# The first expert pair's rows taken by one-hot products on TensorE instead of a gather

## Chip, core and metric

The program runs on one core of a Trainium2 chip. The time is the device time of one execution in microseconds (us); before the change it is 1830.18 us, the median of 3 runs (1829.35 to 1831.33).

## What is computed

Two layers (l = 0, 1), each on x of 512 tokens x 1024 channels in float32. Cut to what matters here, from the reference:

```python
x = x + merged @ w_out[l]
x = x + hier_moe(rmsnorm(x, norm_ffn[l]), router_group[l], ..., expert_gate[l], expert_up[l], expert_down[l])

# in hier_moe: each token goes to the two best of 32 experts (of its best group of 8)
buf = jnp.zeros((cap, D), h.dtype).at[dest].set(ht[tok_sorted])       # rows sorted by expert
out = (jax.nn.silu(xb @ w_gate[e]) * (xb @ w_up[e])) @ w_down[e]      # 1024 -> 512 -> 1024
```

## The kernel before

In each layer an attention and state-space part comes first; then `project_out_and_route` on TensorE forms `merged @ w_out` tile by tile (four tiles of 128 tokens, `out_part`, L1159), and the router works one tile behind it. VectorE adds the product into `x` (`mix_in_x`, L2101), picks the experts (`choose`) and computes for each token and each of its two experts a place: the pair (round and pair of experts, A_) and the slot of 128 in that pair (B_), in `assign`. In the last tile TensorE has nothing else to do between the steps of the router, and runs products whose result nobody reads: `keep_at_work(KEEP[i])` with `KEEP = (4, 3, 6)` (L1209).

The 32 experts are worked in 16 pairs, each with 64 slots of the 128 for each of its two experts. `tabulate` (L1202) sums one-hot products, `slot_hot` by `pair_hot`, into a table of token numbers by slot and pair. VectorE copies it out (L2192) and shifts it (L2194), and GpSimd gathers with column 0 of it the 128 rows of the first pair from `x_rows`, a copy of `x` in device memory that ScalarE's queue has written (L1444, L1448), into `xrow` (`gather`, L690). TensorE then turns the rows, eight transposes of every eighth channel each (`turn_rows`, L1249), VectorE multiplies them by the norm's gain into `xg` (`gain_rows`, L2227), four channel groups at a time, and takes each row's norm factor (`slot_root`, L2224). The expert products are L1266: gate, then up, then down, with the rows as stationary operand and weights as moving one. `xg_ready` counts four steps; the gate products of a pair wait for two of them, and their second half for all four.

Order around the change: every engine has its own program order. TensorE's is: the last tile's products, `leave` (a drain, L559), `experts`, which waits for `rows_in`, turns the rows, reads two numbers from `rounds` into registers (L1321, L1322), enters the loop and starts the gate products. SyncE issues the loads of expert weights. There are ten buffers of 2 MB; loads 0 to 9 fill them before the experts start, load 8 behind `x_out` (the copy of x is written), load 9 behind `rows_in` (the first gather has landed). Load 10 goes into the buffer of load 0 when the first half of the first gate product is done (`gate_free`), and so on (`refill`): 96 loads a layer.

The two points at which an instruction is waited for by name here:

```python
# experts(l), TensorE
pe.wait_ge(rows_in, 16)
turn_rows()
pe.wait_ge(rounds_ready, 1)
nb = pe.value_load(rounds[0:1, 0:1], min_val=1, max_val=MAXR)
# SyncE
sp.wait_ge(rows_in, 16)
load(9, 1)
```

## Time and profile before

| | |
|---|---|
| median of 3 runs | 1830.18 us |
| the profiled execution, its own time | 1827.42 us |
| its span | 1825.6 us |
| TensorE busy | 1647.8 us, 90% |
| VectorE, ScalarE, GpSimd busy | 33%, 23%, 11% |
| read from device memory | 489.25 MB |

The profiled execution took 1827.42 us, of which the span, first to last recorded instruction, is 1825.6. "Busy" of TensorE is not "needed": it counts every row that overlaps. Layer 0 has its change-over from router to experts at 431 to 449 us of the span and its experts until about 890; layer 1 the same at 1335 to 1353 and until about 1800. A row of a timeline holds the start in us, the duration in us, engine, line, operation, operands, count, and in square brackets the idle time before it and who ended it. A float32 product shows as two instructions. L554, L555 and L559 are helper lines (register steps, waits, drain), and PEldq is TensorE's sequencer.

### The profile page before, as it was taken

Reading aid. Unit: us, or ns where it says so; the run is one execution under the profiler, and the core shown is the slowest. Engines: PE = TensorE matmul, PEld = TensorE weight load, DVE = VectorE, ACT = ScalarE, POOL = GpSimd, SP = SyncE. Lnnn points to the kernel's source line nnn. Section 1 sums busy time; section 2 is a strip of 40 time slices with the busy share of each in tenths; the row PEclk is TensorE's granted clock in tenths of the full one; section 3 lists DMA queues with packets and bytes.
Section 4 is the critical chain, followed back from the end, with each engine's and each line's share of the span. In section 5 each row is a group of like instructions: output and inputs, shape, how many; then the busy total and the mean of one; then the engine's idle time right before and its main releaser. Section 6 shows DMA issues by size and latency. Waiting matters only on the chain. (4 is left out here: it accounts for less than half of the span.)

```text
span 1825.6 us, 22382 instructions
## 1 busy us (share of the span) xinstructions
PE 1647.8 (90%) x7764; PEld 863.7 (47%) x7764; DVE 596.4 (33%) x1750; ACT 411.4 (23%) x999; POOL 199.8 (11%) x283
## 2 busy tenths in 40 slices
PE   8999999999998787787999999999999978877778
PEld 6666766454443333333377577654543433323233
DVE  4885356334000000000278844553340000000003
ACT  3323555011111111111122254540111111011110
POOL 0012421000100100000000134210001100000000
PEclk9999999999999998999999999999999998999999
DMA  6631101565999999999947111026569999999998
GB/s 171 145 103 47 47 24 47 207 253 189 415 426 428 427 424 427 427 427 428 392 109 201 47 48 47 24 59 240 220 265 412 426 428 426 424 428 425 429 426 337
DMA packets 122931, 496.44 MB, mean 272 GB/s; under 512 B 42036, under 2 KB 78900, under 8 KB 94160
## 3 DMA queue, kind: packets, MB, share of 16 engines
q1 hardware_dynamic: 110608, 472.75, 65.4%
q0 software_dynamic: 8928, 16.52, 2.4%
q10 hardware_dynamic: 3296, 5.84, 0.8%
q8 instruction: 64, 1.05, 0.2%
q14 instruction: 35, 0.29, 0.0%
HBM read 489.25 MB, written 30.47 MB: 285 GB/s over the span
## 5 line engine op out<-in xcount | busy, mean ns | idle before, releaser
L1266 PE MATMUL bank<-arena 128*64 128x512 f32 x2176 | 684.4, 615 | 97.1 <-DMA arena<-in_expert_up 27.8
L1266 PEld LDWEIGHTS bank<-arena 128*64 128x64 f32 x2176 | 227.7, 141 | 356.8 <-issue 356.7
L2239 DVE SCALAR_TENSOR_TENSOR arena<-bank,halves,arena 128x512 f32<-128x512 f32 x32 | 24.0, 751 | 813.0 <-PE bank L1266 813.0
L1266 PE MATMUL bank<-h,arena 128*64 128x512 f32 x320 | 140.7, 616 | 26.5 <-DMA arena<-in_expert_gate 11.1
L1266 PE MATMUL bank<-spare_slot,arena 128*64 128x512 f32 x320 | 132.3, 611 | 29.6 <-DMA arena<-in_expert_gate 8.5
L891 PE MATMUL bank<-arena,hT 128*128 128x256 f32 (+1 forms) x512 | 119.6, 390 | 3.8 <-DMA arena<-in_w_in 2.9
L1266 PE MATMUL bank<-hT,arena 128*64 128x512 f32 x256 | 118.2, 617 | 0.0
L1159 PE MATMUL bank<-arena,hT 128*128 128x512 f32 x256 | 115.0, 597 | 0.0
L891 PEld LDWEIGHTS bank<-arena,hT 128*128 128x128 f32 x512 | 96.7, 192 | 20.5 <-issue 3.1
L1667 ACT ACT_TABLE_LOAD x32 | 41.1, 1283 | 262.4 <-PE bank L1266 262.4
L915 PE MATMUL bank<-hT,arena 128*128 128x256 f32 x384 | 97.1, 387 | 0.5 <-ACT arena L1510 0.5
L1266 PEld LDWEIGHTS bank<-h,arena 128*64 128x64 f32 x320 | 42.3, 141 | 109.6 <-issue 109.6
L1266 PEld LDWEIGHTS bank<-spare_slot,arena 128*64 128x64 f32 x320 | 40.3, 140 | 105.7 <-issue 105.7
L1669 ACT ACTIVATE arena<-bank 128x512 f32<-128x512 f32 x32 | 19.1, 597 | 295.8 <-PE bank L1303 295.8
L1552 ACT ACTIVATE arena<-bank,nbias 128x32 f32<-128x32 f32 (+4 forms) x192 | 83.4, 447 | 6.4 <-DVE nbias L2046 6.3
L891 PE MATMUL bank<-arena 128*128 128x512 f32 (+1 forms) x216 | 83.7, 551 | 0.0
L915 PEld LDWEIGHTS bank<-hT,arena 128*128 128x128 f32 x384 | 68.4, 191 | 14.8 <-issue 6.2
L915 PE MATMUL bank<-h,arena 128*128 128x256 f32 x288 | 72.0, 386 | 0.7 <-ACT spare_slot L1508 0.7
L1159 PEld LDWEIGHTS bank<-arena,hT 128*128 128x128 f32 x256 | 46.6, 190 | 49.4 <-issue 49.4
L934 PE MATMUL bank<-hT,arena 128*128 128x512 f32 x128 | 68.4, 616 | 1.5 <-ACT arena L1510 1.4
L2046 DVE TENSOR_REDUCE nbias<-bank 128x1 f32<-128x128 f32 (+3 forms) x128 | 54.8, 483 | 44.8 <-PE bank L1090 44.8
L677 POOL TENSOR_TENSOR arena<-arena 128x512 f32<-128x512 f32 x48 | 61.2, 1277 | 1.1
(382 smaller groups left out, 1936.5 us busy)
## 6 DMA issues: line engine op xcount, KB each, us to landing
arena<-in_expert_up SPq DMA_DIRECT2D x48, 2048.0 KB, 38.7
arena<-in_expert_gate SPq DMA_DIRECT2D x44, 2048.0 KB, 34.8
arena<-in_expert_down SPq DMA_DIRECT2D x44, 2048.0 KB, 39.2
arena<-in_w_in SPq DMA_DIRECT2D x26, 1024.0 KB, 5.7
spare_slot<-in_expert_gate SPq DMA_DIRECT2D x8, 2048.0 KB
h<-in_expert_gate SPq DMA_DIRECT2D x8, 2048.0 KB, 32.0
hT<-in_expert_up SPq DMA_DIRECT2D x8, 2048.0 KB, 41.4
spare_slot<-in_expert_down SPq DMA_DIRECT2D x8, 2048.0 KB
```

The lines of the kernel that those rows point to most:

```text
L677: pool.tensor_tensor(out=w[out_], in0=w[x1], in1=w[x2], op=op).then_inc(w_sums, 1)
L891: r = pe.matmul(dst, w, m, start=(i == 0), stop=(i == len(pairs) - 1))
L915: return pe.matmul(dst, w, h, start=(half == 0 and k == 0), stop=(half == 1 and k == KD // 2 - 1))
L934: r = pe.matmul(bank[:, FB, :], lhs, rhs, start=(k == 0), stop=(k == n - 1))
L1159: r = pe.matmul(bank[:, c, :], mergedT[:, k, P * t:P * t + P], w_o[:, c, k, :], start=(k == 0), stop=(k == KD - 1))
L1266: r = pe.matmul(dst[CAP * e:CAP * e + CAP, :], moving[:, k, CAP * e:CAP * e + CAP], w, start=(k == 0), stop=(k == n - 1))
L1552: act.activation(p, s, ACT.Exp, scale=-1.0, bias=nbias[:, n % 2, i:i + 1], accum_out=rsum[:, n % 2, i:i + 1])\
L1667: act.activation(hid, bank[:, 2, :], ACT.Silu, scale=slot_root).then_inc(silu_done, 1)
L1669: act.activation(actT.rearrange("p a b -> p (a b)"), bank[:, 6, :], ACT.Copy).then_inc(at_ready, 1)
L2046: dve.tensor_reduce(nbias[:, n % 2, i:i + 1], bank[:, i, 0:nk], AX.X, ALU.min).then_inc(max_ready, 1)
L2239: STT(hid, bank[:, 3, :], slot_root, hid, ALU.mult, ALU.mult).then_inc(act_ready, 1)
```

## The change

The first pair is no longer gathered. For every tile VectorE computes `first_slot` = 128 A_ + B_, which is below 128 only for places in round 0, pair 0, and from it a one-hot matrix of token by slot, `row_hot`. TensorE multiplies it (as stationary operand) with `x` (moving, 512 wide, in an order that puts channels 8p + k together for each k) over the four tiles, in two halves of the channels, and with the column of norm factors. ScalarE copies both halves to `xrow`, TensorE turns them with eight transposes of neighbouring columns (`turn_first`), VectorE applies the gain. These products stand where `keep_at_work` stood, and `keep_at_work` is gone. The table's last tile, copy and shift come later, since only the second pair needs them. The two numbers of `rounds` are computed and read earlier. `slot_hot` and `pair_hot` have one buffer in place of two, the table's products go to bank 3. Loads 8 and 9 lose their waits. TensorE's wait `enter(pe, exp_clear, l)` stands ahead of `project_out_and_route`. Every other pair is gathered as before.

```diff
@@ GpSimd
                 pool.wait_ge(table_ready, 1)
                 pool.wait_ge(x_out, 32 * NT)
-                gather(table[:, 1, 0:1])
                 pool.wait_ge(xg_ready, 4)
                 gather(table[:, 1, 1:2])
@@ SyncE
                 leave(sp, left_mix)
-                sp.wait_ge(x_out, 32 * NT)
                 load(8, 1)
-                sp.wait_ge(rows_in, 16)
                 load(9, 1)
@@ TensorE
-            def keep_at_work(n):
-
-                for i in range(n):
-                    pe.matmul(bank[:, 3, :], ident[:, :], x[:, i % NT, 0:512], start=True, stop=True)
+            def first_rows(c, *tiles):
+
+                for t in tiles:
+                    pe.wait_ge(hot_ready, t + 1)
+                    r = pe.matmul(bank[:, c, :], row_hot[:, t, :],
+                                  x[:, t, :].rearrange("q (p k) -> q k p", k=KD)[:, 4 * c:4 * c + 4, :],
+                                  start=(t == 0), stop=(t == NT - 1))
+                    if t == NT - 1:
+                        r.then_inc(rows_mm, 1)
+
+            def first_roots(*tiles):
+
+                for t in tiles:
+                    r = pe.matmul(bank[:, 6, P:P + 1], row_hot[:, t, :], row_root[:, t, 0:1],
+                                  start=(t == 0), stop=(t == NT - 1))
+                    if t == NT - 1:
+                        r.then_inc(roots_mm, 1)
+
+            def turn_first(c):
+
+                pe.wait_ge(rows_copied, c + 1)
+                for k in range(4):
+                    o = 512 * c + P * k
+                    r = pe.transpose(bank[:, c, P * k:P * k + P], xrow[:, o:o + P], ident[:, :])
+                r.then_inc(xt_done, 1)
...
                 logits(t, 1)
-                keep_at_work(KEEP[0])
+                first_rows(0, 0, 1, 2)
+                first_rows(1, 0)
                 prefix(t)
-                keep_at_work(KEEP[1])
-                tabulate(t)
-                keep_at_work(KEEP[2])
+                first_rows(1, 1, 2)
+                first_roots(0, 1, 2)
+                first_rows(0, t)
+                first_rows(1, t)
+                first_roots(t)
...
-                pe.wait_ge(rows_in, 16)
-                turn_rows()
                 pe.wait_ge(rounds_ready, 1)
                 nb = pe.value_load(rounds[0:1, 0:1], min_val=1, max_val=MAXR)
                 earlier = pe.value_load(rounds[0:1, 1:2], min_val=0, max_val=PAIRS * (MAXR - 1))
+                turn_first(0)
+                tabulate(NT - 1)
+                turn_first(1)
@@ ScalarE
+                for c in range(2):
+                    act.wait_ge(rows_mm, c + 1)
+                    act.activation(xrow[:, 512 * c:512 * c + 512], bank[:, c, :], ACT.Copy).then_inc(rows_copied, 1)
                 act.wait_ge(r_exp_in, 1)
@@ VectorE
                     do(STT(pl(A_), pl(ROUND_), float(PAIRS), pl(PAIR), ALU.mult, ALU.add))
+                    do(STT(first_slot[:, t, :], pl(A_), float(P), pl(B_), ALU.mult, ALU.add))
+                    do(TS(row_hot[:, t, :], iota_f[:, :], first_slot[:, t, 0:1], None, ALU.is_equal))
+                    STT(row_hot[:, t, :], iota_f[:, :], first_slot[:, t, 1:2], row_hot[:, t, :], ALU.is_equal, ALU.add)\
+                        .then_inc(hot_ready, 1)
...
+                one_hots(NT - 1)
+                dve.wait_ge(roots_mm, 1)
+                dve.tensor_copy(slot_root, bank[:, 6, P:P + 1]).then_inc(xg_ready, 1)
+                dve.wait_ge(xt_done, 1)
+                gain_rows(0)
+                dve.wait_ge(table_mm, NT)
...
+                dve.wait_ge(xt_done, 2)
+                dve.sem_inc(xg_ready, 1)
+                gain_rows(1)
+                TS(table[:, 1, :], table[:, 0, :], 1, None, ALU.logical_shift_right).then_inc(table_ready, 1)
```

TensorE's order between the last `prefix` and the first expert product, first before (L1209 the idle products, L1202 the table, L1249 the transposes of the gathered rows, L1321 and L1322 the register loads):

```order
L1209 MATMUL bank<-x,ident 128x512 x3
L1202 MATMUL bank<-arena 128x128 [waits slots_ready] x2
L1209 MATMUL bank<-x,ident 128x512 x6
L1249 MATMUL bank<-ident,arena 128x128 [waits exp_clear,rows_in]
L1249 MATMUL bank<-ident,arena 128x128 x7
L1321 TENSOR_LOAD rounds [waits rounds_ready]
L1321 ISA x2
L1322 TENSOR_LOAD rounds
L1322 ISA x2
L1323 UNCONDITIONAL_BRANCH
L1323 ISA
L554 ISA [waits xg_ready]
```

The same stretch of the changed kernel (L1212 `first_rows`, L1221 `first_roots`, L1345 and L1346 the register loads, L1231 `turn_first`, L1204 the table):

```order
L1212 MATMUL bank<-x,arena 128x512 [waits hot_ready] x2
L1221 MATMUL bank<-arena 128x1
L1345 TENSOR_LOAD rounds [waits rounds_ready]
L1345 ISA x2
L1346 TENSOR_LOAD rounds
L1346 ISA x2
L1231 MATMUL bank<-ident,arena 128x128 [waits rows_copied]
L1231 MATMUL bank<-ident,arena 128x128 x3
L1204 MATMUL bank<-arena 128x128 [waits slots_ready] x2
L1231 MATMUL bank<-ident,arena 128x128 [waits rows_copied]
L1231 MATMUL bank<-ident,arena 128x128 x3
L1350 UNCONDITIONAL_BRANCH
```

The register loads have moved ahead of the transposes, and the table's last tile between the two groups of transposes.

VectorE's order behind the last `assign`, before (L2168, L2170 `slot_hot` and `pair_hot`):

```order
L2166 SCALAR_TENSOR_TENSOR place<-place 128x2
L2168 TENSOR_SCALAR arena<-iota_f,place 128x128 [waits dve_chain]
L2170 TENSOR_SCALAR arena<-iota_f,place,row_f 128x128
L2168 TENSOR_SCALAR arena<-iota_f,place 128x128
L2170 TENSOR_SCALAR arena<-iota_f,place,row_f 128x128
L2190 TENSOR_REDUCE cnt<-bank 128x1
L2192 TENSOR_SCALAR table<-bank 128x128 [waits table_mm,dve_chain]
```

And of the changed kernel (L2196 to L2198 the new one-hot, L2206 and L2208 the old two):

```order
L2195 SCALAR_TENSOR_TENSOR place<-place 128x2
L2196 SCALAR_TENSOR_TENSOR first_slot<-place 128x2 [waits dve_chain]
L2197 TENSOR_SCALAR arena<-iota_f,first_slot 128x128 [waits dve_chain]
L2198 SCALAR_TENSOR_TENSOR arena<-iota_f,first_slot,arena 128x128 [waits dve_chain]
L2233 TENSOR_REDUCE cnt<-bank 128x1
L2234 TENSOR_SCALAR cnt<-thr,cnt 128x8 [waits dve_chain]
L2235 TENSOR_REDUCE cnt<-cnt 128x1 [waits dve_chain]
L2236 TENSOR_SCALAR cnt<-cnt 128x1 [waits dve_chain]
L2237 TENSOR_SCALAR cnt<-cnt 128x1
L2238 CAST rounds<-cnt 128x2 [waits dve_chain]
L2206 TENSOR_SCALAR arena<-iota_f,place 128x128 [waits table_mm]
L2208 TENSOR_SCALAR arena<-iota_f,place,row_f 128x128
```

The new one-hot comes first, then the round numbers, and only then the operands of the table.

## Rows read from the trace of the kernel before

**Rows 1.** Windows: length, PE, PEld, DVE, ACT, POOL busy, PEclk, DMA share, GB/s

```profile
458.00:474.00 16.00, 14.58 (x72) 6.40 (x70) 2.01 (x4) 1.79 (x3) 1.24 (x3) 1.00 1.00 427
474.00:880.00 406.00, 335.82 (x1502) 136.63 (x1500) 28.09 (x56) 52.07 (x69) 32.73 (x54) 0.95 1.01 425
```

**Rows 2.** The chain that ended last, layer 1's experts: start us, us, what

```profile
1441.88 13.97 PE bank L1266 x64
1456.50 39.46 DMA arena<-in_expert_down
...
1732.22 42.69 DMA arena<-in_expert_down
```

**Rows 3.** Timeline of SyncE's queue, layer 0: loads 8, 9, 10, and 14 with 15

```profile
436.54 0.33 SPq L809 DMA_DIRECT2D arena<-in_expert_up  x1
446.08 0.33 SPq L809 DMA_DIRECT2D hT<-in_expert_up  x1
452.82 0.36 SPq L809 DMA_DIRECT2D spare_slot<-in_expert_down  x1
...
473.17 0.84 SPq L809 DMA_DIRECT2D arena<-in_expert_up  x2
```

**Rows 4.** Timeline of TensorE, the change-over of layer 0, and last of layer 1

```profile
434.05 3.68 PE L1209 MATMUL bank<-x,ident 128*128 128x512 f32 x8
...
437.93 2.82 PE L1209 MATMUL bank<-x,ident 128*128 128x512 f32 x6
...
446.62 1.14 PE L1249 MATMUL bank<-ident,arena 128*128 128x128 f32 x8 [0.26 <-issue]
448.75 3.65 PE L1266 MATMUL bank<-spare_slot,arena 128*64 128x512 f32 x16 [1.00 <-DVE arena L2227]
...
1352.42 3.65 PE L1266 MATMUL bank<-spare_slot,arena 128*64 128x512 f32 x16 [0.80 <-DVE halves L2224]
```

**Rows 5.** TensorE's sequencer by line, 430 to 460 us: ns, start us

```profile
L559 PEldq DRAIN  x1: 5598/5598/5598, 440.8 to 440.8; - x1
...
L1321 PEldq TENSOR_LOAD <-rounds x1: 489/489/489, 446.7 to 446.7; - x1
...
L1322 PEldq SEQ_ASSERT  x1: 18/18/18, 448.1 to 448.1; - x1
```

**Rows 6.** Timeline of VectorE in layer 0's last two tiles

```profile
412.61 0.69 DVE L2101 SCALAR_TENSOR_TENSOR x<-bank,x 128x512 f32<-128x512 f32 x1 [1.88 <-PE bank L1159]
...
439.20 0.17 DVE L2164 TENSOR_SCALAR place<-place 128x2 f32<-128x2 f32 x1
439.40 0.16 DVE L2165 SCALAR_TENSOR_TENSOR place<-place 128x2 f32<-128x2 f32 x1
...
439.67 0.29 DVE L2168 TENSOR_SCALAR arena<-iota_f,place 128x128 f32<-128x128 f32 x1
...
440.32 0.34 DVE L2170 TENSOR_SCALAR arena<-iota_f,place,row_f 128x128 f32<-128x128 f32 x1
...
447.34 0.69 DVE L2227 TENSOR_TENSOR arena<-bank,g_ffn 128x512 f32<-128x512 f32 x1 [1.67 <-PE bank L1249]
```

**Rows 7.** ScalarE's copies of a bank, by line: ns min/median/max

```profile
L1440 ACT ACTIVATE arena<-bank x14: 591/597/597, 381.3 to 1331.4; 128x512 f32<-128x512 f32 x14
```

**Rows 8.** Weight loads by line and shape: busy us, mean ns of one

```profile
L1249 PEld LDWEIGHTS bank<-ident,arena 128*128 128x128 f32 x256 | 31.0, 193 | 26.4 <-issue 24.3 <-DMA arena<-x_rows,table 2.1
...
L1118 PEld LDWEIGHTS bank<-arena,h 128*64 128x64 f32 x320 | 16.7, 135 | 23.2 <-DVE arena L2072 14.0 <-issue 5.4 <-ACT arena L1562 2.7
...
L975 PEld LDWEIGHTS bank<-arena 128*63 128x63 f32 x128 | 10.3, 205 | 20.2 <-issue 20.2
...
L1170 PEld LDWEIGHTS bank<-ident,x 128*128 128x128 f32 x64 | 7.5, 141 | 5.3 <-issue 4.2 <-DVE x L2101 1.1
```

**Rows 9.** Windows around one pair's transposes, and TensorE behind a long wait

```profile
484.00:490.00 6.00, 4.50 (x26) 2.37 (x23) 2.01 (x4) 0.60 (x1) 0.18 (x1) 1.00 1.02 434
...
603.64 1.08 PE L1266 MATMUL bank<-h,arena 128*64 128x512 f32 x1 [3.03 <-DMA arena<-in_expert_gate]
```

More of the change, by code:

```diff
@@ L70 @@
 NRING = 4
-KEEP = (4, 3, 6)
 PLAIN = 2
@@ L306, in trunk @@
         junk = view(112, 512)
-        slot_hot = view(107, 2, 2, P)
-        pair_hot = view(109, 2, 2, P)
+        slot_hot = view(107, 2, P)
+        pair_hot = view(108, 2, P)
+        row_hot = view(109, NT, P)
         ident = sb("ident", [P, P])
@@ L358, in trunk @@
         table = sb("table", [P, 2, P], I32)
+        first_slot = sb("first_slot", [P, NT, 2])
         slot_tok = sb("slot_tok", [P, 1], I32)
@@ L448, in trunk @@
         member_ready = sem("member_ready")
-        slots_ready = sem("slots_ready")
-        table_mm = sem("table_mm")
+        slots_ready = sem("slots_ready", "exp")
+        table_mm = sem("table_mm", "exp")
+        hot_ready = sem("hot_ready", "exp")
+        rows_mm = sem("rows_mm", "exp")
+        roots_mm = sem("roots_mm", "exp")
+        rows_copied = sem("rows_copied", "exp")
         table_ready = sem("table_ready", "exp")
@@ L727, in _ @@
                 pool.sem_inc(yslot_free, 1)
-                wait_reg(pool, rows_in, earlier * 16 + 16 * PAIRS)
+                wait_reg(pool, rows_in, earlier * 16 + 16 * (PAIRS - 1))
                 pool.dma_reset()
@@ L1298, in pair @@
                     else:
-                        wait_reg(pe, rows_in, it * 16 + 32)
+                        wait_reg(pe, rows_in, it * 16 + 16)
                         turn_rows()
@@ L1660, in _ @@
                 leave(act, left_mix)
+                act.wait_ge(x_out, 32 * NT)
                 act.wait_ge(rounds_ready, 1)
@@ L2183, in _ @@
                         assign(t - 1)
+                        one_hots(t - 1)
                     mix_in_x(t, 1)
@@ L2190, in _ @@
                 do(dve.tensor_reduce(cnt[:, 8:9], bank[:, 6 + (NT - 1) % 2, 96:96 + NE], AX.X, ALU.max))
-                dve.wait_ge(table_mm, NT)
-                do(TS(table[:, 0, :].rearrange("p (h w v) -> p h w v", h=4, w=4),
-                      bank[:, 2, 0:P].rearrange("p (h v w) -> p h w v", h=4, w=4), float(EMPTY), None, ALU.add))
-                TS(table[:, 1, :], table[:, 0, :], 1, None, ALU.logical_shift_right).then_inc(table_ready, 1)
                 do(TS(cnt[:, 0:8], thr[:, :], cnt[:, 8:9], None, ALU.is_lt))
@@ L2197, in _ @@
                 link(TS(cnt[:, 10:11], cnt[:, 9:10], 1.0, None, ALU.add))
+                do(TS(cnt[:, 11:12], cnt[:, 9:10], float(PAIRS), None, ALU.mult))
+                dve.tensor_copy(rounds[:, :], cnt[:, 10:12]).then_inc(rounds_ready, 1)
+                one_hots(NT - 1)
[4 more added lines that the diff above has]
+                dve.wait_ge(table_mm, NT)
+                do(TS(table[:, 0, :].rearrange("p (h w v) -> p h w v", h=4, w=4),
+                      bank[:, 3, 0:P].rearrange("p (h v w) -> p h w v", h=4, w=4), float(EMPTY), None, ALU.add))
+                dve.wait_ge(xt_done, 2)
+                dve.sem_inc(xg_ready, 1)
+                gain_rows(1)
+                TS(table[:, 1, :], table[:, 0, :], 1, None, ALU.logical_shift_right).then_inc(table_ready, 1)
                 link(TS(cnt[:, 12:13], cnt[:, 9:10], float(PAIRS), float(PAIRS - 1), ALU.mult, ALU.add))
-                do(TS(cnt[:, 11:12], cnt[:, 9:10], float(PAIRS), None, ALU.mult))
-                dve.sem_inc(xg_ready, 1)
-                dve.tensor_copy(rounds[:, :], cnt[:, 10:12]).then_inc(rounds_ready, 1)
                 for t in range(NT):
@@ L2224, in root_rows @@
                     dve.tensor_copy(slot_root, xrow[:, D:D + 1]).then_inc(xg_ready, 1)
-                def gain_rows(q):
-                    TT(xg[:, 4 * q:4 * q + 4, :], bank[:, q, :].rearrange("p (k c) -> p k c", k=4),
-                       bc(g_ffn[:, 4 * q:4 * q + 4], P), ALU.mult).then_inc(xg_ready, 1)
-                for q in range(2):
-                    dve.wait_ge(xt_done, q + 1)
-                    gain_rows(q)
-                    if q == 0:
-                        root_rows()
                 def gated(it):
```

16 lines of the change are left out of this document (10 added, 6 removed).

## Prediction

> **What bounds the kernel now.** I read four views, from the whole to the place. The windows first: in layer 0's experts the DMA engines are busy at 1.00 of their time and move 427 GB/s from 458 us on, and 425 GB/s for the next 406 us, while TensorE is busy for 336 of those 406 [rows 1]. So the experts' end is set by when the stream of weights gets going, not by TensorE's speed in the middle. The chain that ended last says the same: TensorE's products up to 1456 us, and from there to the last load at 1732 one DMA wait after another, 39 to 43 us from issue to landing [rows 2], which is the time that a full set of buffers takes.
>
> What starts that stream is in SyncE's queue. Loads 0 to 9 fill the ten buffers. Load 10 is issued at 452.82, four microseconds behind the first gate product at 448.75 [rows 3, 4], because it needs the buffer that the first half of that product frees. Loads 14 and 15 come at 473.17, when pair 0 is done. From load 10 on 86 loads are still to be moved, whatever happened before. If the first expert product starts a given time earlier, load 10 and all releases of pair 0 do too, and the layer ends that much earlier. Layer 1 has the same structure, with its first expert product at 1352.42. So the question is what ends last before 448.75.
>
> Load 9 is issued when the first gather has landed: 446.08 [rows 3]. But the idle products end only with the drain, at 440.8 + 5.6 = 446.4 [rows 5]. The transposes start at 446.62 [rows 4]. TensorE's sequencer reads the two numbers from 446.7 to 448.1 [rows 5], and the first gate product starts at 448.75. VectorE's gain, 447.34 + 0.69 = 448.03 [rows 6], was there 0.7 earlier. So the chain is: router, table, gather (with the idle products 0.3 longer still), transposes issued, register loads (1.4), loop entry (0.6).
>
> **The change, part by part.**
>
> VectorE. Before, the one-hots start at 439.67 [rows 6]. Now `first_slot` stands there, a small dependent operation: 0.20, the distance of two such (439.20 to 439.40). Then a 128-wide comparison whose end is waited for, 0.29 and some 0.04, and a 128-wide one with two tensor inputs, which the trace does not show with this operation; I take 0.34, the dearer 128-wide row [rows 6]; between 0.29 and 0.69 (a 512-wide one) it can cost 0.05 less or 0.35 more. `hot_ready` comes at 439.67 + 0.20 + 0.33 + 0.34 = 440.54. In the earlier tiles these 0.9 us fall into VectorE's wait for TensorE, 1.88 us in the row shown [rows 6]; were it gone, they would cost 0.9 three times a layer.
>
> TensorE, hidden part. The idle products were 4, 3 and 6; now four products with `x` stand ahead of `prefix`, two and three small ones behind it. At equal speed four take the same 3.68 us up to 437.7, and two (1.9) with three small ones (six instructions of about 0.12, the eight transposes' pace of 1.14 / 8 [rows 4], 0.7) end at 437.93 + 2.6 = 440.5, just when `hot_ready` comes. Cost nothing, with 0 to 0.1 us to spare.
>
> TensorE, exposed part. Two 512-wide products after `hot_ready`: 8 instructions in 3.68 us make 0.44 each [rows 4], so the first half ends at about 440.6 + 1.1 = 441.7, the second at 442.6, the small one at 442.9. There the drain ends, 3.5 us before the old one.
>
> ScalarE copies each half in 0.60 [rows 7], to 442.4 and 443.3. Hidden behind TensorE's sequencer: from the end of the drain it takes 0.3 to the first register load and 1.4 for both, as before [rows 5]: 442.9 + 1.7 = 444.6. Without that cover the second copy would end the chain here, at 443.3.
>
> Transposes: four, two table products (four instructions), four; twelve at 0.14 are 1.7 us, to 446.3; the first group is through at 445.3. VectorE's gain follows, 0.1 + 0.69 [rows 6], to 446.1. The first gate product needs both: 446.2. Loop entry (0.6 before) is passed by the sequencer meanwhile; if not, add 0.3. Against 448.75 this is **2.55 us earlier per layer, 5.1 in all**; with layer 1's start at 1352.42, whose gap behind its own release was 0.2 shorter (0.80 against 1.00 of idle time [rows 4]), I take 2.45 there: 5.0.
>
> What else moves costs nothing. Loads 8 and 9 come earlier, at 436.5 or before; they are not needed before pair 1, and do not change load 10. The table's copy and shift are late by about 5 us, so the second pair's rows are fetched at about 447.5 instead of 449.5, and are used when pair 0's up products end, some 14 us after its start. The router's softmax on VectorE and ScalarE moves behind the gain, some 4 us later; the next work there is the activation after the 32 gate instructions, 7 us (twice 3.65 [rows 4]) after the start, at 453. The gather removed is 0.5 MB out of 200 per layer: under 1.3 us of the DMA engines at 427 GB/s, and in a stretch where they have room.
>
> **The disputed price: `x` read in steps of eight.** `first_rows` streams `x` with a step of 8 floats, 32 bytes. No matmul row of before has such a moving operand. For stationary operands there are rows [rows 8]: transposes load neighbouring columns in 141 ns (L1170) and every eighth in 193 (L1249); products load 64 neighbouring columns in 135 ns (L1118) and 63 of every eighth in 205 (L975). So steps cost 52 ns for 128 columns and about 70 for 63. A moving stream has 0.44 us for 512 columns, 0.86 ns each. L1249 reads its 128 columns in steps at no worse a pace than one in 0.14 us, 1.1 ns each, and perhaps at 0.9; so the lower bound is no loss, factor 1.0. Taking L975's extra, 1.1 ns per column, on top of 0.86 gives 2.3: the upper bound. L975's loads come in pairs to two halves of the array and may hinder each other, and L1249's 52 ns for 128 columns is only 0.4 ns each; I hold 1.0 to 1.1 as the likelier, but not by much.
>
> The Trainium skill speaks against the change here: Advanced Engine Details and Errata, section Memory Cachelines, says that SBUF lines are 16 bytes and that an access to a different line each time has a penalty, at least two hits on a line being needed to hide it. By that rule each float of `x` lies on a line of its own, and the sum would be that of the second rival below. The weight loads agree with the rule for stationary operands; no row here shows it for a moving one.
>
> **Rivals.**
>
> 1. *Forecast.* Stride free, clock full: 1827.42 - 5.0 = 1822.4 for a profiled execution. It stood 2.8 us below the median, so the median becomes 1825.2. Own range 1823.0 to 1827.5, from the loop entry, the one-hot's price and the register loads. Chance 0.50.
>
> 2. *The stream in steps runs at half pace (other side).* Place: `first_rows`. At twice the time the first four products end at 434.05 + 7.4 = 441.4, then `prefix`; behind it two products and the small ones, 0.2 + 3.7 + 0.7, to 446.0 (`hot_ready`, 2.8 behind `prefix`, is at 444.3 and no longer last); the last two 3.5 and the small one: 449.7. With 3.3 from the drain to the first gate product this is 453.0, 4.2 later than before and 8.4 in both layers: 1838.6. All eight products then lie on the chain, about 6.8 us for a doubling; it breaks even near a factor of 1.4. For it: L975 and the rule. Against: L1249's pace. Chance 0.25.
>
> 3. *Something between*, factor 1.15 to 1.5, mostly because weight loads and stream share the reading: 1827 to 1831. Chance 0.13.
>
> 4. *The clock.* The idle products kept TensorE at full clock. Now it has gaps: 442.9 to 446.2 has transposes and table only. Behind an idle time of 3.03 us an expert product took 1.08 us instead of 0.6 [rows 9], that is the 1.2 GHz level; a few of these cost 1.3 to 3 us. Against: in the window 484 to 490, where a pair's twelve transposes and the wait behind them lie, TensorE is busy for 4.50 of 6.00 us, and PEclk stays 1.00 [rows 9]. If the clock falls at both layers: 1822.4 + 4 = 1826.4 profiled, 1829 as the median. Chance 0.08.
>
> 5. *No carry*: the start moves and the stream does not, say because load 10's buffer is not what is missing. Against: rows 3 show load 10 right behind the product's first half. 1830. Chance 0.04.
>
> **The numbers.** 1825.2 from case 1. The measurement tells some 0.2% apart, 3.7 us, so faster means below 1826.5: most of case 1 and a little of 3, 0.48. Within 0.2%: the rest of 1, most of 3, 4 and 5, 0.25. Slower: case 2 and the end of 3, 0.27. For 8 in 10 the range must reach into case 2: 1823 to 1839, of which case 1 alone fills 1823 to 1827.5.
>
> **What would show it.** Right: L1212 rows of 0.6 us at 0.43 distance, TensorE's drain ending near 443, first L1292 near 446.2 and 1350, load 10 near 450.3, the DMA share at 1.00 from about 456, no PEclk below 1.00 from 440 to 452. Rival 2: L1212 rows of 1 us and more, `prefix` near 441. Rival 4: L1292's first rows at 1.08. Wrong otherwise: a first gate product at 446.2 with the layer's end unmoved.

## The result and the profile after

The changed kernel takes 1837.62 us, the median of 6 runs (1835.64 to 1838.78); the kernel before, on the same chip, 1828.57 (1826.85 to 1831.33). The ratio is 1.0053 with a 95% interval of 1.0043 to 1.0064: slower by 0.53%, some 9.7 us (the two medians themselves are 9.1 apart). The forecast was 1825.2. It is the second rival that happened, whose time was 1838.6.

The profiled execution has a span of 1835.3 us, 9.7 more than before; 488.19 MB are read in place of 489.25. The same views, in the order of the prediction. First TensorE's timeline at the change-over of layer 0, which answers to [rows 4]:

```profile
433.64 7.58 PE L1212 MATMUL bank<-x,arena 128*128 128x512 f32 x8
441.04 0.25 PE L1192 MATMUL bank<-member,ones_h 128*128 128x32 bf16 x3
...
441.26 3.90 PE L1212 MATMUL bank<-x,arena 128*128 128x512 f32 x4
...
445.58 3.90 PE L1212 MATMUL bank<-x,arena 128*128 128x512 f32 x4
...
451.35 0.65 PE L1231 MATMUL bank<-ident,arena 128*128 128x128 f32 x4 [1.75 <-issue]
451.84 1.02 PE L1204 MATMUL bank<-arena 128*128 128x128 f32 x4
452.65 1.06 PE L1231 MATMUL bank<-ident,arena 128*128 128x128 f32 x4
453.65 4.45 PE L1292 MATMUL bank<-spare_slot,arena 128*64 128x512 f32 x16
```

The first eight product instructions take 7.58 us where the eight idle ones took 3.68 [rows 4]. `prefix` stands at 441.04, the first gate product at 453.65 and not at 446.2. Up to the products this execution runs 0.4 us ahead of the one before (433.64 against 434.05), so the gate product is 5.3 us later, measured from there; in layer 1 it is 5.8 (1363.08 less 1342.84, against 1352.42 less 1337.96).

The products by line (ns, minimum/median/maximum), and TensorE's sequencer, which answers to [rows 5]:

```profile
L1212 PE MATMUL bank<-x,arena x32: 1097/1098/1142, 433.6 to 1357.6; 128*128 128x512 f32 x32
```

```profile
L564 PEldq DRAIN  x1: 5738/5738/5738, 443.9 to 443.9; - x1
...
L1345 PEldq TENSOR_LOAD <-rounds x1: 482/482/482, 449.8 to 449.8; - x1
...
L1346 PEldq SEQ_ASSERT  x1: 18/18/18, 451.3 to 451.3; - x1
```

All 32 are near 1.1 us. The drain ends at 443.9 + 5.74 = 449.6, and the register reads cost their 1.7 us behind it, as forecast. VectorE, which answers to [rows 6]:

```profile
441.52 0.29 DVE L2178 TENSOR_TENSOR arena<-arena,bank 128x32 f32<-128x32 f32 x2 [3.99 <-PE bank L1196]
...
443.17 0.29 DVE L2197 TENSOR_SCALAR arena<-iota_f,first_slot 128x128 f32<-128x128 f32 x1
443.49 0.35 DVE L2198 SCALAR_TENSOR_TENSOR arena<-iota_f,first_slot,arena 128x128 f32<-128x128 f32 x1
```

VectorE stands 3.99 us before it can use `prefix`. Its last one-hot is there at 443.84, while TensorE works on its earlier products until 445.6: TensorE's stream is what ends last, all the way. SyncE's queue answers to [rows 3], and the windows (length, busy time of PE, PEld, DVE, ACT, POOL, then PEclk, DMA share, GB/s) to [rows 1] and [rows 9]:

```profile
430.70 0.33 SPq L813 DMA_DIRECT2D arena<-in_expert_up  x1
431.15 0.36 SPq L813 DMA_DIRECT2D hT<-in_expert_up  x1
458.51 0.36 SPq L813 DMA_DIRECT2D spare_slot<-in_expert_down  x1
```

```profile
435.00:438.00 3.00, 3.00 (x4) 0.93 (x3) 2.29 (x14) 0.00 (x0) 0.00 (x0) 0.50 0.97 397
439.00:442.00 3.00, 3.00 (x12) 0.82 (x11) 0.48 (x5) 0.00 (x0) 0.00 (x0) 1.00 1.07 454
449.00:455.00 6.00, 4.25 (x19) 2.71 (x19) 2.29 (x9) 1.88 (x2) 0.00 (x0) 0.74 0.00 0
...
474.00:880.00 406.00, 330.16 (x1506) 135.24 (x1504) 28.09 (x56) 52.67 (x70) 32.85 (x54) 0.97 1.01 425
```

Loads 8 and 9 are early, load 10 is 5.7 us later than before, and from 449 to 455 the DMA engines move nothing at all. From 474 on the stream has its 425 GB/s as before. In the third window the granted clock is 0.74: it fell to its lower level some half a microsecond behind the end of the 1.75 us wait (in layer 1 within the wait of 1.54), so that the table's products took 1.02 us and the first sixteen gate instructions 4.45 (3.65 in [rows 4]). The chain that ended last is of the same kind as in [rows 2], DMA waits of some 41 us each:

```profile
1703.16 41.38 DMA arena<-in_expert_up
```

### The profile page after: what moved, and what is told of

Its sections match the earlier page's. It is cut to its first block and busy times, and to the rows that moved or that the text cites. A ratio compares the mean times of both kernels' runs of the same rounds, so it can differ in the third digit from the quotient of the medians.

```text
span 1835.3 us, 22404 instructions
## 1 busy us (share of the span) xinstructions
PE 1661.0 (91%) x7760; PEld 862.8 (47%) x7760; DVE 602.6 (33%) x1774; ACT 413.8 (23%) x1003; POOL 198.2 (11%) x281
## 3 DMA queue, kind: packets, MB, share of 16 engines
HBM read 488.19 MB, written 30.47 MB: 283 GB/s over the span
```

## The experiments

### The pace of a moving operand by its step

Only the idle products of the kernel before are changed:

```diff
+                flat = x.rearrange("p t d -> p (t d)")
                 for i in range(n):
-                    pe.matmul(bank[:, 3, :], ident[:, :], x[:, i % NT, 0:512], start=True, stop=True)
+                    s = (1, 2, 4, 8, 3, 6)[i]
+                    pe.matmul(bank[:, 3, :], ident[:, :], flat[:, 0:511 * s + 1:s], start=True, stop=True)
```

> The kernel before, with nothing changed but the idle products L1209 (their result is read by nobody, so nothing of the computation is left out): their moving operand, 512 columns of x, is read in steps of 1, 2, 4, 8, 3 and 6 floats in turn. The changed kernel's instructions with step 8 took 0.917 us each where step 1 takes 0.44. Theory A, the cost starts where each float lies on a line of 16 bytes of its own: steps 1 and 2 stay at 0.43 to 0.44 us per instruction, steps 4, 6 and 8 go to about 0.92, step 3 to 0.92 or somewhat less. Theory B, any step but 1 costs the same: step 2 is at 0.92 as well. Theory C, it is not the step but the one-hot as stationary operand, or the product's four-part order of columns: all six stay at 0.43 to 0.44. The idle products grow by A from 5.7 to about 9 us in the last group, so the first expert product comes some 2 us later in each layer and the time is 3 to 6 us above before; by C it is unchanged.

One instruction of each step from the last group of products, in the order 1, 2, 4, 8, 3, 6 (ns, and its start):

```profile
L1211 PE MATMUL bank<-x,ident x1: 595/595/595, 442.8 to 442.8; 128*128 128x512 f32 x1
L1211 PE MATMUL bank<-x,ident x1: 612/612/612, 444.1 to 444.1; 128*128 128x512 f32 x1
L1211 PE MATMUL bank<-x,ident x1: 1057/1057/1057, 444.5 to 444.5; 128*128 128x512 f32 x1
L1211 PE MATMUL bank<-x,ident x1: 1098/1098/1098, 446.3 to 446.3; 128*128 128x512 f32 x1
L1211 PE MATMUL bank<-x,ident x1: 854/854/854, 448.1 to 448.1; 128*128 128x512 f32 x1
L1211 PE MATMUL bank<-x,ident x1: 1072/1072/1072, 450.4 to 450.4; 128*128 128x512 f32 x1
```

From start to start it is 0.44 us at steps 1 and 2, 0.7 at step 3, and 0.9 at 4, 6 and 8. Theory A holds; B falls at step 2. C falls too: a plain identity as stationary operand and one single pass over the columns show the same 1.1 us that the one-hots had. The one run of this kernel took 1837.4 us against a median of 1826.77 before, 10.6 more. That is above the 3 to 6 I expected: I had counted only the last group's growth (from 5.3 to 8.7 us), but the first and second group are on the chain too (5.63 and 3.80 us in place of 3.68 and 2.82), as VectorE waits for `prefix` behind the first one. Slow products alone, with the gather still there, make about as much time as the whole change did.

### Steps or lines of 16 bytes

```diff
+                    g = flat.rearrange("p (n k) -> p n k", k=8)
+                    m = [g[:, 0:256, 0:2], g[:, 0:256, 3:5], g[:, 0:128, 0:4],
+                         x[:, 0, :].rearrange("q (p k) -> q k p", k=KD)[:, 0:4, :],
+                         g[:, 0:128, 2:6], flat[:, 1:513]][i]
+                    pe.matmul(bank[:, 3, :], ident[:, :], m, start=True, stop=True)
```

> The kernel before, with only the idle products' moving operand changed again (their result is read by nobody). The run with steps gave 0.44 us per instruction at steps 1 and 2, 0.69 at step 3 and 0.9 at 4, 6 and 8. Now six orders of 512 floats of x in turn: two neighbours of every eight (floats 0, 1); two neighbours of every eight that lie on either side of a multiple of four (floats 3, 4); four neighbours of every eight (0 to 3); the changed kernel's own order (every eighth, four passes of 128); four of every eight from float 2 on (2 to 5); and 512 neighbours from float 1 on. Theory A, what counts is whether two floats read one after the other lie on the same 16 bytes: 0.44, 0.9, 0.44, 0.9, 0.44 and 0.44. Theory B, what counts is the jump between columns, so that any break in the row costs: the pairs, straddling or not, the same 0.6 to 0.7, the fours 0.55. Theory C, the mean number of bytes passed over counts (every eight floats holding two costs as step 4 does): pairs of both kinds at 0.9, fours at 0.44 as step 2. The two kinds of pairs tell A from the others. The Trainium skill, Advanced Engine Details and Errata, section Memory Cachelines, gives lines of 16 bytes, which is A.

One instruction of each in that order (the third, the fours, is from the middle group):

```profile
L1214 PE MATMUL bank<-x,ident x1: 624/624/624, 443.4 to 443.4; 128*128 128x512 f32 x1
L1214 PE MATMUL bank<-x,ident x1: 1059/1059/1059, 444.3 to 444.3; 128*128 128x512 f32 x1
L1214 PE MATMUL bank<-x,ident x1: 590/590/590, 442.5 to 442.5; 128*128 128x512 f32 x1
L1214 PE MATMUL bank<-x,ident x1: 1101/1101/1101, 447.9 to 447.9; 128*128 128x512 f32 x1
L1214 PE MATMUL bank<-x,ident x1: 631/631/631, 448.8 to 448.8; 128*128 128x512 f32 x1
L1214 PE MATMUL bank<-x,ident x1: 592/592/592, 450.1 to 450.1; 128*128 128x512 f32 x1
```

The two kinds of pairs have the same jumps and the same number of floats passed over. The pair (0, 1) costs 624 ns, the pair (3, 4), which lies on either side of a multiple of four floats, 1059; from start to start that is 0.46 and 0.9 us. This is theory A: what counts is whether the next float lies on the same 16 bytes as the last. The Trainium skill, Advanced Engine Details and Errata, section Memory Cachelines, says so: lines are 16 bytes, and at least two hits on a line are needed to hide the access. The trace agrees, down to step 3, where some neighbours share a line and some don't (0.7 us).

The twelve readings also give a price, as an estimate. At steps 4 to 8 each of the 512 floats lies on a line of its own, and 0.9 us over 512 lines is 1.75 ns per line. Step 3 touches 384 lines: 0.67 us by this price, 0.67 to 0.69 measured. Step 2 and the pair (0, 1) touch 256: 0.45 us, about the 0.44 that 512 neighbouring floats take in any case.

The one run of this kernel took 1836.64 us against a median of 1825.89 before.

### The change with neighbouring columns

The step goes from the stream of 512 columns to the stationary side of the transposes, where [rows 8] had its price.

```diff
@@ first_rows
-                                  x[:, t, :].rearrange("q (p k) -> q k p", k=KD)[:, 4 * c:4 * c + 4, :],
+                                  x[:, t, 512 * c:512 * c + 512],
@@ turn_first
-                pe.wait_ge(rows_copied, c + 1)
+                pe.wait_ge(rows_copied, 2)
-                    r = pe.transpose(bank[:, c, P * k:P * k + P], xrow[:, o:o + P], ident[:, :])
+                    r = pe.transpose(bank[:, c, P * k:P * k + P], xrow[:, 4 * c + k:D:KD], ident[:, :])
```

> The changed kernel with one thing different: the products with the one-hots read neighbouring columns of x, 512 at a time, so that the rows come out in plain order, and the transposes pick every eighth channel from xrow and wait for both copies. Theory A, the step of the moving operand is what made the change slow, and the clock's fall behind it follows from it: products at 0.44 us, prefix near 437.5, TensorE's drain ending near 442.5, transposes from about 444.3, first gate product near 446.3 and 1349.9, load 10 near 450.5; the kernel is 3.5 to 5 us faster than before, ratio 0.9972 to 0.9981, and 13 to 15 us faster than the changed kernel. Theory B, the clock falls by itself once the idle products are gone (gaps while ScalarE copies): products at 0.44, but first gate products at 0.53 us and more per instruction and the granted clock below 1.00 from about 445 on; some 2 us per layer of the gain are lost, ratio near 1.000. Theory C, the removed gather and the early loads 8 and 9 cost in the stream of weights: start earlier as in A, end not earlier, ratio 1.000 and above.

Measured: 1822.05 us (1819.89 to 1825.32) against 1826.77; ratio 0.9970 (0.9960 to 0.9981). This is theory A (0.9972 to 0.9981 was expected): some 5.5 us faster than before and 15 faster than the change as it was. TensorE in layer 1, and one line of layer 0:

```profile
1336.37 3.68 PE L1212 MATMUL bank<-x,arena 128*128 128x512 f32 x8
...
1342.88 1.98 PE L1212 MATMUL bank<-x,arena 128*128 128x512 f32 x4
...
1346.44 0.71 PE L1230 MATMUL bank<-ident,arena 128*128 128x128 f32 x4 [1.46 <-ACT arena L1684]
...
1348.27 3.65 PE L1291 MATMUL bank<-spare_slot,arena 128*64 128x512 f32 x16 [0.24 <-DVEq L2247]
```

```profile
433.47 5.38 PE L1212 MATMUL bank<-x,arena 128*128 128x512 f32 x8
```

From the first product to the first gate product it is 11.90 us in layer 1; the forecast had 446.2 - 434.05 = 12.15. In layer 0 it is 13.73, since the same eight instructions took 5.38 us: there the granted clock was 0.50 from 434 to 437. On the short side the step costs little: the weight loads of the sixteen transposes took 188 ns in the median, against 140 for those of neighbouring columns in the run that fills the gap, below.

### Register reads ahead of the drain

```diff
                 pe.wait_ge(rounds_ready, 1)
                 nb = pe.value_load(rounds[0:1, 0:1], min_val=1, max_val=MAXR)
                 earlier = pe.value_load(rounds[0:1, 1:2], min_val=0, max_val=PAIRS * (MAXR - 1))
+                leave(pe, left_mix)
                 turn_first(0)
```

(and `leave` is gone behind `project_out_and_route`)

> As the run before it (plain columns), and TensorE reads its two numbers of rounds into registers ahead of its drain instead of behind it, while it still works on the last products. If the drain and the register reads stand one behind the other on the chain (0.3 and 1.4 us in the trace), the transposes then wait for the second copy of the rows alone, and the first gate product comes 0.7 to 1.4 us earlier than in the run before, in each layer: 1.4 to 2.8 us in all, ratio to the kernel before 0.996 to 0.997. Rival: the second copy ends last already (drain near 442.5, copies to 443.3, the transposes 0.1 later), and the register reads are hidden behind it but for about 1 us: 0.5 us per layer or less. Rival on the other side: the numbers are not ready when TensorE's sequencer comes to them, so that the last products are issued late: no faster or slower than the run before.

Measured: 1820.05 us (1817.3 to 1824.0), ratio 0.9962 (0.9948 to 0.9975). The transposes now wait 0.57 us, and for ScalarE's copy:

```profile
443.61 0.71 PE L1230 MATMUL bank<-ident,arena 128*128 128x128 f32 x4 [0.57 <-ACT arena L1684]
...
445.45 3.65 PE L1291 MATMUL bank<-spare_slot,arena 128*64 128x512 f32 x16 [0.24 <-DVEq L2247]
```

The gap was 1.75 and 1.46 in the two layers of the run before, so 0.9 to 1.2 us per layer are saved, as the trace has it, within the 0.7 to 1.4 that I expected. The two intervals overlap, so the times alone do not tell the two versions apart. The clock fell in both layers here (5.38 us for the first eight instructions).

### Loads 8 and 9 early, alone

```diff
-                sp.wait_ge(x_out, 32 * NT)
                 load(8, 1)
-                sp.wait_ge(rows_in, 16)
                 load(9, 1)
```

> The kernel before, and only loads 8 and 9 of each layer lose their waits, as in the change. In the changed kernel load 10 came 6.1 us later than before and the layer ended 4.9 to 5.3 later, so about 0.8 us per layer came back somewhere. Theory A: the early loads give it back, since two buffers less have to be filled beside load 10: this kernel is 0.8 to 1 us per layer faster, 1.6 to 2 us in all (ratio 0.9990). Theory B: the engines of the DMA are not short of work before load 10, and the early loads change nothing: within 0.5 us. Theory C: they collide with the transfers of x and of the rows, the gather lands later, and it is slower.

Measured: 1838.39 us (1834.96 to 1840.05), ratio 1.0056 (1.0041 to 1.0071): theory C, for which I had given no size. TensorE:

```profile
450.31 1.97 PE L1247 MATMUL bank<-ident,arena 128*128 128x128 f32 x8 [4.21 <-DMA arena<-x_rows,table]
452.55 5.76 PE L1264 MATMUL bank<-spare_slot,arena 128*64 128x512 f32 x16 [0.28 <-DVE halves L2222]
```

GpSimd's gather, of this kernel and of the one before:

```profile
446.96 1.23 POOL L690 DMA_INDIRECT arena<-x_rows,table  x1 [120.27 <-DMA x_rows<-arena]
```

```profile
442.78 1.23 POOL L690 DMA_INDIRECT arena<-x_rows,table  x1 [115.84 <-DVE table L2194]
```

And the last tile's copy of x among the DMA issues of 430 to 452 us (KB each, median us from issue to landing), again of this kernel and of the one before:

```profile
x_rows<-x ACTq DMA_DIRECT2D x1, 512.0 KB, 11.8
```

```profile
x_rows<-x ACTq DMA_DIRECT2D x1, 512.0 KB, 2.6
```

With 4 MB of weights under way, the last tile's copy of x took 11.8 us in place of 2.6, and the 8 KB of norm factors issued behind it 12.4 in place of 2.6. The gather reads both. Before, it started when the table was ready; here it waits for the factors and starts 4.2 us later. The experts start 4 us late, on a lowered clock (0.50 from 452 to 456). Those two waits were no idle caution: they kept the way free for the gather. Which of the two matters was not tried. In the change they went together with the first gather; the last experiment asks whether that is harmless.

### What the fallen clock costs the change

Two products that nobody reads fill the wait behind the drain, in the changed kernel with its step of eight:

```diff
+                for n in (512, 384):
+                    pe.matmul(bank[:, 2, 0:n], ident[:, :], x[:, 0, 0:n], start=True, stop=True)
                 pe.wait_ge(rounds_ready, 1)
```

> The changed kernel with its step of eight as it is, and two products whose result nobody reads (512 and 384 columns, 1.5 us) behind TensorE's drain, in the 1.75 us in which it waited for its register reads (nothing of the computation is left out). In the changed kernel's trace the granted clock is at its lower level from 451.8 on, the table's products took 1.02 us instead of 0.61, four transposes 1.06 instead of 0.60, the first sixteen gate instructions 4.45 instead of 3.65. Theory A: the gap lets the clock fall, and with the gap filled the transposes, table and gate run at full clock: 0.4 + 0.4 + 0.8 and a little, some 1.7 us per layer, 3.4 in all, ratio to the kernel before 1.0035 in place of 1.0053. Theory B: the fall comes from the products with a step of eight, which keep TensorE at half its pace for 15 us, and the filling changes nothing, or delays the transposes by up to 0.2 per layer: ratio 1.005 to 1.0055.

```profile
448.68 1.77 PE L1345 MATMUL bank<-x,ident 128*128 128x512 f32 x4
450.29 0.60 PE L1231 MATMUL bank<-ident,arena 128*128 128x128 f32 x4
...
451.17 0.60 PE L1231 MATMUL bank<-ident,arena 128*128 128x128 f32 x4
452.01 3.65 PE L1292 MATMUL bank<-spare_slot,arena 128*64 128x512 f32 x16 [0.25 <-DVEq L2250]
```

In the trace it is theory A: from the fill on the granted clock is 1.00 in both layers, and load 10 is 1.4 and 0.9 us nearer to the first product, 2.3 in place of the 3.4 that theory A had. In the times nothing is seen: 1836.63 us (1835.93 to 1838.01), ratio 1.0054 (1.0040 to 1.0067), against 1.0053 for the change. This is the number of theory B, and theory A's 1.0035 lies outside the interval. A gain of 2.3 us still lies within what two such ratios can differ by; whether it is there stays open.

The wait alone does not lower the clock. The plain version has a wait of the same length at the same place:

```profile
445.37 0.70 PE L1230 MATMUL bank<-ident,arena 128*128 128x128 f32 x4 [1.75 <-issue]
```

There the granted clock stayed at 1.00 behind it, in both layers. The slow products alone did not lower it either: in the two kernels with stepped idle products, where the wait behind them was 0.2 to 0.3 us, it stayed at 1.00. Of these kernels only the changed one, which has both, the slow products and behind them a wait of 1.5 to 1.75 us, saw it fall there, in both layers.

### The fill ahead of the logits

```diff
                 turn_x(t, 1)
+                pe.matmul(bank[:, 2, 0:384], ident[:, :], x[:, 0, 0:384], start=True, stop=True)
                 logits(t, 1)
```

> The fastest version so far (plain columns, register reads ahead of the drain, 1820.05 us), with one product of 384 columns that nobody reads (0.66 us) in the 0.78 us in which TensorE waits for the last half of xT ahead of the logits. In that version's trace the granted clock fell just behind the logits in both layers, and the first four products with one-hots took 5.38 us in place of 3.68, 1.7 us per layer. In the kernel before it did not fall there, though TensorE had the same waits. Theory A: the wait is what lets it fall, and filling it keeps the clock: 3.68 in both layers, the first gate product up to 1.7 earlier, 0 to 3.4 us in all, ratio 0.9945 to 0.996. Theory B: whether it falls is set by something else in the run, and this product does not decide it: 5.38 in one layer or both, ratio 0.996 to 0.997. On the other side, if the product delays the logits, 0.1 us per layer is lost.

Measured: 1819.41 us (1818.55 to 1822.23), ratio 0.9960 (0.9948 to 0.9973), the lowest of all, though not told apart from 0.9962 without the fill. The first eight instructions take 3.68 in both layers, and the first gate product comes 11.0 us behind the first product:

```profile
431.74 0.81 PE L1260 MATMUL bank<-x,ident 128*128 128x384 f32 x2
...
433.60 3.68 PE L1212 MATMUL bank<-x,arena 128*128 128x512 f32 x8
...
444.62 3.65 PE L1292 MATMUL bank<-spare_slot,arena 128*64 128x512 f32 x16 [0.24 <-DVEq L2248]
```

In this profile and in that of the last experiment the clock stays up in all four layers; in the two plain versions without the fill it fell in three of four. That the fill did it is likely but not shown: in kernels with idle products at the places of before it stayed up without one in nine layers of ten. The ratio is where theory A and theory B meet and does not decide.

### The register reads in the kernel before

```diff
-KEEP = (4, 3, 6)
+KEEP = (4, 3, 5)
@@ experts
-                pe.wait_ge(rows_in, 16)
-                turn_rows()
                 pe.wait_ge(rounds_ready, 1)
 ...
+                leave(pe, left_mix)
+                pe.wait_ge(rows_in, 16)
+                turn_rows()
```

(`leave` is gone behind `project_out_and_route`, and the wait for `exp_clear` stands ahead of it, as in the change)

> The kernel before, with its gather, and only TensorE's register reads moved ahead of the drain (and its wait for exp_clear ahead of the router), and one idle product less at the end (KEEP = 4, 3, 5), so that the drain ends at 445.5 and not at 446.4. How much of the gain of the plain version is to be had without the change? The transposes can then start when the gather has landed (load 9's issue at 446.1 shows when), VectorE's gain follows 0.7 + 0.7 later, and the first gate product stands at 447.8 in place of 448.75: theory A, 0.9 us per layer, 1.8 in all, ratio 0.999. Theory B: the gather lands later than it seems for TensorE, and the gap before the transposes lets the clock fall: no gain, or up to 2 us per layer lost, ratio 1.000 to 1.002.

Measured: 1825.15 us (1824.26 to 1829.07) against 1825.89, ratio 0.9995 (0.9986 to 1.0004): the interval holds theory A's 0.999 and the 1.000 of theory B, so the times do not decide. In layer 0 the first gate product is 13.88 us behind the first product, 0.8 nearer than in [rows 4]. In layer 1 the products that are those of the kernel before took

```profile
1336.82 5.38 PE L1209 MATMUL bank<-x,ident 128*128 128x512 f32 x8
```

at a granted clock of 0.50 from 1337 to 1340, so the fall of the clock behind the logits can happen in the order of before as well. There the first gate product came 15.49 us behind the first product, 1.0 later than in the kernel before.

### No idle products

`KEEP = (0, 0, 0)` in the kernel before.

> The kernel before without its idle products (KEEP = 0, 0, 0; nobody reads their result). What were they worth, and so what does the gap cost that the change could have opened? TensorE then has about 12 us behind the logits with only prefix and table in them. Theory A: the clock is at its lower level when the experts start. The run with early loads shows the price behind a gap of 4.2 us: eight transposes 1.97 us in place of 1.14, the first sixteen gate instructions 5.76 in place of 3.65, 2.9 us together; against that the drain no longer ends after the gather (0.3 to 0.5 us). So 2.4 us per layer, 4.8 in all, ratio 1.002 to 1.003. Theory B: VectorE's and the gather's times set everything and TensorE catches up: load 10 at the same place, ratio 1.000. On the other side: without them prefix and table could come earlier (VectorE waited 0.28 us for prefix), at most 0.3 us per layer.

```profile
445.43 1.97 PE L1249 MATMUL bank<-ident,arena 128*128 128x128 f32 x8 [4.91 <-DMA arena<-x_rows,table]
447.68 5.51 PE L1266 MATMUL bank<-spare_slot,arena 128*64 128x512 f32 x16 [0.28 <-DVE halves L2224]
```

Measured: 1828.64 us (1826.21 to 1831.08) against 1826.60, ratio 1.0012 (1.0003 to 1.0022). Theory A, at half its size in the time (2.2 us of 4.8) and three quarters of it in the trace: the first gate product itself comes no later in layer 0 and 0.2 us later in layer 1, and load 10 comes 1.8 us later in each, as the first product is slow.

### Loads 8 and 9 held back in the fastest version

```diff
                 leave(sp, left_mix)
+                sp.wait_ge(x_out, 32 * NT)
                 load(8, 1)
```

> The fastest version so far (plain columns, register reads first, the small product ahead of the logits; 1819.4 us), with loads 8 and 9 held back again until the copy of x is written. With the gather in the chain the early loads cost 5 us a layer: the copy of x took 11.8 us from issue to landing in place of 2.6, and the gather behind it came 4.2 us late. Theory A: in the changed kernel nothing on the chain reads device memory before the first expert product, so early or late loads make no difference: load 10 at the same distance from the logits (15.9 us), ratio 0.996 as before, within 1 us of it. Theory B: the early loads use an idle stretch of the DMA engines, and held back they cost 0.5 to 1.5 us a layer: ratio 0.9966 to 0.9975. Theory C: they delay the copy of x and with it the second pair's gather, so that held back they gain: ratio under 0.9955.

Measured: 1819.71 us (1818.73 to 1820.88), ratio 0.9965 (0.9952 to 0.9977), load 10 at 15.08 us behind the first product against 15.09: theory A by the trace. In the time nothing is seen between this and 0.9960, but the interval also holds the 0.5 to 1.5 us a layer of theory B.

### All of them on one scale

Load 10's issue less the start of the first product behind the last logits, layer 0 and layer 1 (without idle products, the place 0.92 us behind the logits' start, where that product would be); the change of the two layers' sum; and the measured change, from the ratio and 1827 us (from one run where there is only one).

| kernel | layer 0 | layer 1 | sum, change | time, change |
|---|---|---|---|---|
| before | 18.77 | 18.52 | | |
| the change | 24.87 | 24.36 | +11.9 | +9.7 |
| steps | 24.92 | 24.70 | +12.3 | +10.6 |
| lines | 23.56 | 23.34 | +9.6 | +10.8 |
| loads 8, 9 early | 24.93 | 23.34 | +11.0 | +10.2 |
| change, gap filled | 23.47 | 23.44 | +9.6 | +9.9 |
| no idle products | 20.56 | 20.32 | +3.6 | +2.2 |
| before, reads first | 17.94 | 19.55 | +0.2 | -0.9 |
| plain | 17.79 | 15.96 | -3.5 | -5.5 |
| plain, reads first | 16.62 | 16.62 | -4.1 | -6.9 |
| with fill | 15.09 | 15.08 | -7.1 | -7.3 |
| loads 8, 9 held back | 15.08 | 15.07 | -7.1 | -6.4 |

The intervals of the last column are 1.6 to 2.7 us to either side; the two kernels with one run, steps and lines, have none. Eleven kernels with quite different edits lie near one line of slope one, the farthest 2.8 us off it: the time hangs on when the first expert product frees load 10's buffer, and that carries through to the end. The layer columns are of one execution, in which the clock fell or not; the last column is of several where there are several.

## Why the prediction was wrong

The step that failed is the disputed price, the term for the two exposed products and for the hidden ones ahead of them. I held the stream in steps of eight at a factor of 1.0 to 1.1, "but not by much", by the pace of L1249's weight loads. The runs showed 0.92 us per instruction against 0.44, a factor of 2.1, far above the 1.4 at which the sum breaks even. The four products ahead of `prefix` then take 7.58 us in place of 3.68, and nothing of the stream is hidden any more.

Where the error lay: the row did not say what I took from it. L1249's pace in steps, 0.14 us for 128 columns, is 1.1 ns per column against the stream's 0.86, a factor of 1.3 already; the "perhaps at 0.9" that made it 1.0 had no row behind it. The other row, L975's 1.1 ns more for each column, gave 2.3, and I set it aside with a reason that no row bore out. Measured is 0.92 - 0.44 us over 512 columns, 0.94 ns more for each. But the same difference at L1249 is 52 ns over 128 columns, 0.4 ns each. The two rows disagreed, both are of stationary operands, and no run shows why L975 came out near. The Trainium skill's rule (Advanced Engine Details and Errata, section Memory Cachelines) names a penalty and no price. The prediction quoted it and went against it; the runs agree with the rule.

The second rival had the mechanism, and its sum is right in its parts: the first four products 7.58 us (7.4 forecast), the drain's end at 449.6, 16.0 behind the first product (449.7 and 15.65), all eight products on the chain. That its 1838.6 stands so near 1837.62 is in part luck. It starts from a median of 1830.18, and the median of six runs before is 1828.57. It puts the gate product 4.2 us later per layer, and it came 5.3 and 5.8 later, mostly since the clock fell behind the drain. And load 10 was 11.9 us later in both layers together, of which 9.7 arrived in the time. The range of 1823 to 1839 holds the measured time only because it was drawn into this rival.

The other steps, one by one.

- The chain of before and what a start is worth: right. Table above.
- VectorE: right. `hot_ready` was forecast at 440.54, 6.49 behind the first product; in the run with fill it is 6.46 (439.71 + 0.35 - 433.60). The operation with two tensor inputs took 0.35 (0.34 taken).
- TensorE at equal pace: right. First gate product 12.15 behind the first product by the forecast, 11.90 in layer 1 of the plain version, though its transposes read in steps.
- Register reads, 1.7 us behind the drain: right, and they need not be there.
- Loads 8 and 9 "cost nothing": nothing is seen in the change, but for a reason that I had not given, that no gather stands behind them there. With the gather in place they cost 5 us a layer.
- The gather's bytes cost nothing: nothing seen, 425 GB/s before and after.
- The clock: a rival of its own with 0.08, and it came on top of the second. In layer 0 it took 4.0 us from the drain to the gate product (3.3 forecast), and the first sixteen gate instructions were 0.8 slower. Its price was set at 2 us per layer; the trace gives 1.4 and 0.9. In the times it is not seen.

So the idea of the change was sound, and its layout was not: with the same products on neighbouring columns the kernel is 5.5 us faster (3.5 to 7.3), against the 5.0 forecast.

## What to carry to other kernels

TensorE's float32 moving operand should take at least two floats, one after the other, from each 16 bytes that it touches: below that it took up to 2.1 times as long here. Where an order of channels has to be made, make it on the short side (the transposes' stationary operand, 128 columns at a time, 48 ns more per load) and not on the stream of 512. Before a wait is taken from a prefetch, ask who else uses the DMA engines then: early loads cost 10 us with a gather behind them and nothing that could be seen without. And where the trace has only distant rows for a new price and they disagree, the price is open: measure it alone, as the first experiment does, or lay the change out so that it is not needed, as the plain version does.

## What the runs showed that I had not expected

- The pace of the products in steps of eight does not follow the clock: in the changed kernel the granted clock was 0.50 from 435 to 438 and 1.00 from 439 to 442, and all its instructions took 1.10 to 1.14 us. Plain ones, in layer 0 of the plain version, took 1.06 at the lower level and 0.59 at the upper.
- The granted clock fell just behind the last logits in some executions and not in others with the same work ahead of it: in the plain version in layer 0 and not in layer 1, in the version with reads first in both, in the changed kernel, with its gap filled and without, in layer 0 alone (where it cost nothing, by the point above), with the fill in none of four, and in the profiles of the kernel before and of the four kernels with idle products at its places once in ten layers. TensorE's longest wait just before was 0.8 us in all of these without the fill. What decides it was not found.
- Two register reads behind a drain cost TensorE 1.7 us, from the drain's end at 449.6 to the last read's at 451.3, if they stand on the chain. Ahead of the drain they left a wait of 0.57 us, which was ScalarE's copy.
- A 512 KB copy took 11.8 us in place of 2.6, and an 8 KB one 12.4 in place of 2.6, behind two loads of 2 MB.
